# The last projection tile takes its feature blocks in another order, and attention's first score units run inside it

## What is computed

```python
h = rms_norm(x, norm_mix_g)
proj = h @ w_in                      # attention q,k,v (512 each); delta-rule q,k,v,z (512 each); gates
a_out = rms_norm(chunked_band_attention(rms_norm(a_q), rms_norm(a_k), a_v, rel_bias))   # 8 heads of 64
d_q, d_k, d_v = silu(causal_conv4(d_qkv))
o = gated_delta_rule(l2norm(d_q), l2norm(d_k), d_v, beta, alpha)      # 4 heads of 128, serial over chunks
d_out = rms_norm(o) * silu(z)
x = x + concat(a_out, d_out) @ w_out
h = rms_norm(x, norm_ffn_g)
x = x + (silu(h @ w_gate) * (h @ w_up)) @ w_down                      # hidden width 2816
```

## Time and profile before

| what | us |
| --- | --- |
| median of 3 runs | 1337.23 |
| lowest and highest | 1332.9 and 1340.54 |
| the profiled execution, its device time | 1330.42 |
| its span in the profile | 1328.7 |
| mean granted TensorE clock | 0.994 of full speed |

### The profile page before, as it was taken

How to read it: one execution, slowest core, us unless ns; L and a number is a source line. 1 busy time by engine, 2 the same in 40 slices (tenths; PEclk the granted TensorE clock), 3 DMA queues, 4 the chain that set the end, 5 groups by cost and what they waited for, 6 DMA issues and landing times.

```text
span 1328.7 us, 18375 instructions
## 1 busy us (share of the span) xinstructions
PE 1284.2 (97%) x6940; PEld 1072.0 (81%) x6940; DVE 745.0 (56%) x1033; ACT 577.9 (43%) x928; POOL 750.6 (56%) x516
## 2 busy tenths in 40 slices
PE   7999999999989989899988999999999999999999
PEld 7888888888878768888867877888888888788887
DVE  6455654536526667745479675664556557344552
ACT  5577655562136654552253323333333233464441
POOL 4332455633229992223068979888787894474541
PEclk9999999999999999999989999999999999999999
DMA  5611355431251004633111534334444336986663
GB/s 207 244 43 36 101 155 145 133 97 32 52 174 45 2 16 143 219 128 115 64 64 64 181 152 166 137 126 182 182 183 154 151 147 214 333 274 200 198 196 144
DMA packets 77807, 186.11 MB, mean 140 GB/s; under 512 B 20680, under 2 KB 24848, under 8 KB 70680
## 3 DMA queue, kind: packets, MB, share of 16 engines
q1 hardware_dynamic: 72144, 180.71, 40.1%
q10 hardware_dynamic: 5576, 4.23, 1.1%
HBM read 130.59 MB, written 56.94 MB: 141 GB/s over the span
## 4 chain that ended last, share of the span: by engine, by line
PE 75%; POOL 7%; DVE 6%; ACT 4%; DMA 4%; issue 3%; SPq 1%; DVEq 0%; ACTq 0%; POOLq 0%
PE ps L1988 24%; PE ps L340 20%; PE ps L2013 13%; PE ps L351 6%; POOL SX L841 2%; PE ps L1820 2%; PE ps L1852 1%; DMA RAWD<-w_down 1%; PE ps L1912 1%; PE ps L1835 1%; PE ps L325 1%; PE ps L1801 1%; POOL WR L740 1%; DMA RAB<-down_t 1%; POOL WX L740 1%
## 5 line engine op out<-in xcount | busy, mean ns | idle before, releaser
L340 PE MATMUL ps<-HT,SPLIT 128*128 128x512 f32 (+1 forms) x1488 | 329.1, 379 | 0.4 <-POOL SPLIT L290 0.4
L340 PEld LDWEIGHTS ps<-HT,SPLIT 128*128 128x128 f32 x1488 | 265.9, 189 | 49.7 <-issue 0.5
L2013 PE MATMUL ps<-S,HI 128*128 128x512 f32 x616 | 190.0, 390 | 1.6 <-POOL S L885 1.3
L885 POOL TENSOR_TENSOR S<-RAB,S 128x512 fp32r<-128x512 f32 x77 | 106.8, 1390 | 95.2 <-ACT S L1056 95.0
L288 POOL CAST SPLIT<-RAW 128x1024 fp32r<-128x1024 f32 x31 | 33.5, 1080 | 186.9 <-PE ps L340 181.9
L2013 PEld LDWEIGHTS ps<-S,HI 128*128 128x128 f32 x616 | 115.5, 188 | 26.5 <-issue 1.7
L1988 PE MATMUL ps<-HI,WR 128*128 128x512 f32 x368 | 119.6, 395 | 5.5 <-ACT UV L1021 5.4
L2013 PE MATMUL ps<-S,LO 128*128 128x512 f32 x308 | 119.8, 389 | 0.0
L1529 DVE TENSOR_TENSOR LO<-RAB,HI 128x512 fp32r<-128x512 f32 x77 | 65.4, 859 | 94.5 <-ACT HI L1053 94.4
L1988 PE MATMUL ps<-S,WR 128*128 128x512 f32 x504 | 117.8, 389 | 0.0
L1988 PE MATMUL ps<-HI,WX 128*128 128x512 f32 x336 | 110.4, 390 | 4.2 <-DVE UV L1467 2.0
(11 more groups left out here) (262 smaller groups left out, 2496.7 us busy)
## 6 DMA issues: line engine op xcount, KB each, us to landing
hidden<-HB SPq DMA_DIRECT2D x11, 1792.0 KB, 6.6
RAB<-hidden SPq DMA_DIRECT2D x77, 256.0 KB, 3.2
RAW<-units SPq DMA_DIRECT2D x37, 512.0 KB, 4.0
RAWG<-w_gate SPq DMA_DIRECT2D x11, 1024.0 KB, 10.9
RAWU<-w_up SPq DMA_DIRECT2D x11, 1024.0 KB, 5.0
RAWD<-w_down SPq DMA_DIRECT2D x11, 1024.0 KB, 8.9
down_t<-RAWD SPq DMA_DIRECT2D x11, 1024.0 KB, 3.9
RAB<-down_t SPq DMA_DIRECT2D x44, 256.0 KB, 3.6
```

Of the source, the lines that this page charges most:

```text
L340: mm = pe.matmul(ps[:, bank + a // HALF, a % HALF:a % HALF + width], w, right[other][:, k, a:a + width], start=(k == 0 and part == 0 and o ...
L885: pool.tensor_tensor(down_b(q, 1), RAB[:, q % RAWS, 1, :], down_b(q, 0).bitcast(F32), ALU.subtract).then_inc(R["b_lo"], 1)
L2013: mm = pe.matmul(ps[:, bank + t, :], down_a(q, part)[:, t * P:(t + 1) * P], down_b(q, other), start=(p == 0 and i in (1, 6, 5, 7) and part ...
```

## The change

It has five parts. (1) `columns_unit` takes an `order` of the feature blocks, and can raise a semaphore after block 7. (2) The last tile is made by a new function `project_last` with the order 3, 4, 5, 6, 7, 0, 1, 2; scores(0) goes ahead of block 0 and scores(1) ahead of block 1, and the semaphore `room` goes up after block 7. (3) DVE begins attention at `room`. (4) ScalarE copies the last tile from PSUM after the exponentials of unit 1, in place of a Silu ahead of attention, and applies Silu in place (SBUF to SBUF) after attention's last PT copy; PE waits for the banks between scores(2) and turn(0). (5) DVE's `att_acc(dve, 2)` moves from ahead of the STATE memset to behind the two masked copies of `dn_dve(0)`, and the first use of the z tiles waits for the late Silu.

```diff
-        def columns_unit(pe, slot, bank, right, first=0, end=T, between={}):
+        def columns_unit(pe, slot, bank, right, first=0, end=T, between={}, order=range(KT), read=None):
...
-            for k in range(KT):
+            for k in order:
...
-                                           start=(k == 0 and part == 0 and other == 0),
-                                           stop=(k == KT - 1 and part == 1))
+                                           start=(k == order[0] and part == 0 and other == 0),
+                                           stop=(k == order[-1] and part == 1))
+                if read is not None and k == KT - 1:
+                    mm.then_inc(read, 1)
...
-                for t in range(Z0, NPROJ):
+                for t in range(Z0, NPROJ - 1):
...
+                    if v == 1:
+                        act.wait_ge(unit_used, U_OUT)
+                        act.activation(proj_banks(NPROJ - 1), bank_pair(slot_of(NPROJ - 1), 4), ACT.Copy).then_inc(banks_free, 1)
...
+                act.wait_ge(banks_free, U_OUT + BANKS0)
+                act.activation(proj_tile(NPROJ - 1), proj_tile(NPROJ - 1), ACT.Silu).then_inc(proj_final, 1)
                 act.wait_ge(A["ao"], NPAIR * NT + AO0)
                 att_square(act, 3)
...
+                if m == 0:
+                    dve.wait_ge(proj_final, SQ0 + 1)
...
                 if m >= 1:
                     dn_dve_r(dve, m - 1)
+                else:
+                    att_acc(dve, 2)
...
-                dve.wait_ge(unit_used, U_OUT)
+                dve.wait_ge(A["room"], 1)
...
                 dve.wait_ge(A["ao"], NPAIR * NT + AO0)
-                att_acc(dve, 2)
                 dve.memset(STATE[:, :, :], 0.0).then_inc(S["st"], 4)
...
+            def project_last(pe):
+                t = NPROJ - 1
+                pe.wait_ge(split_done, U_TILE + t + 1)
+                pe.wait_ge(banks_free, U_TILE + t + 1)
+                columns_unit(pe, slot_of(t), 4 + 2 * slot_of(t), HTP, 0, T,
+                             {0: lambda: att_scores(pe, 0), 1: lambda: att_scores(pe, 1)},
+                             (3, 4, 5, 6, 7, 0, 1, 2), A["room"]).then_inc(unit_used, 1)
...
-                for t in range(SDV + 1, NPROJ):
+                for t in range(SDV + 1, NPROJ - 1):
...
-                att_scores(pe, 0)
-                att_scores(pe, 1)
-                pe.wait_ge(banks_free, U_OUT + BANKS0)
+                project_last(pe)
                 for v in range(NV):
                     if v + 2 < NV:
                         att_scores(pe, v + 2)
+                    if v == 0:
+                        pe.wait_ge(banks_free, U_OUT + BANKS0)
                     att_turn(pe, v)
```

More of the change, by code:

```diff
@@ L364, in hymba_block @@
         A = {n: sem("att_" + n) for n in
-             ("acc", "gt_turned", "masked", "scores", "biased", "prob", "turned", "pt0", "pt1", "pv", "inv", "scaled", "ao",
+             ("room", "acc", "gt_turned", "masked", "scores", "biased", "prob", "turned", "pt0", "pt1", "pv", "inv", "scaled", "ao",
               "sq", "sums", "ln", "rs", "mix")}
```

## The result

| | median us | lowest to highest | runs |
| --- | --- | --- | --- |
| before | 1335.75 | 1332.6 to 1340.54 | 6 |
| changed | 1326.1 | 1324.67 to 1326.65 | 6 |

The ratio is 0.9932, with a 95% interval of 0.9911 to 0.9953. By it the change takes 9.1 us (6.3 to 11.9) off. I had said 6.1, just outside that interval. The measured time lies inside the stated range, near its fast end. The profiled execution of the changed kernel took 1324.67 us, span 1322.9, against a span of 1328.7 before: 5.8 us. So the two profiles differ by less than the medians do, and both numbers have to be explained.

The account below looks back on a forecast made before the run. PE, busy in 97% of the span, bounds the kernel, so time comes only from its waits or slow stretches. Gains of 4.2 + 1.9 = 6.1 us take the median from 1337.23 to 1331.1 us, range 1325.5 to 1337.

Parts of the forecast that it names:

- First turn: Projection to attention: with scores inside the last tile, scores(3) ends 4.2 us earlier (bounds 2.5 and 4.7).
- a pause of 0.47 for the copy: Projection to attention: PE was to stand 0.5 us before turn(0) for ACT's copy of the last tile.
- idle weight loads: Last projection tile: PE's weight loads idle 0.17 us at each of two switches between scores and projection.
- both PE and POOL move by the same time: Attention: both engines gain 4.2 us at its start, so its end moves by as much.
- Second turn: Attention to delta rule: later sum of squares brings first TT addition 2.0 us earlier; 1.9 taken, bounds 0.7 and 2.8.
- The lock: Attention to delta rule: DVE's sum of squares is blocked until POOL's subtract ends; without this, gain near 3 us.
- 1.3 us to spare: Attention to delta rule: ACT's square could come 1.3 us later, against a possible 1.2 us delay from table switching.
- 1324.3 forecast: Whole kernel: the profiled execution's 1330.42 us less the gain of 6.1 us.
- (a): First turn pays, second doesn't, as clock falls or DVE's sum ends later: gain 3 to 4.9 us; chance 0.15.
- (b): Delta rule: a load of UT keeps its old time and swallows the shift; gain 0 to 2 us; chance 0.12.
- (c): Attention to delta rule: DVE's sum waits for POOL, TT begins 5.9 us later; 1.7 us slower overall; chance 0.05.
- (d): Clock stays up at second turn and switches cost nothing: gain 4.7 + 2.8 = 7.5 us or more; chance 0.13.

Follow-up runs that it names:

- e7: Changed kernel with scores(0) and scores(1) each one block later in the last tile: 1327.23 us, ratio to before 0.9953.
- e6: Changed kernel with POOL's second weight unit held until DVE's sum of squares is done: 1324.94 us, ratio to before 0.9930.
- e2: Kernel before with only DVE's sum of squares moved behind the two masked copies: 1329.75 us, ratio to before 0.9966.
- e4: Changed kernel with DVE's sum of squares one step later, behind both additions to TT: 1324.24 us, ratio to before 0.9929.
- e12: Kernel before run once more without any edit, a single run for a second profile: 1334.09 us.
- e3: The changed kernel run again without further edit, beside its parts on the same chip: 1325.39 us, ratio to before 0.9934.
- e11: e1 plus 12 matmuls of the identity that nobody reads, in PE's pause from attention to delta rule: 1323.72 us, ratio to before 0.9924.
- e1: Changed kernel with DVE's sum of squares put back ahead of the STATE memset: 1330.85 us, ratio to before 0.9976.
- e5: Kernel before with 9 and 12 unread identity matmuls in PE's pauses at the two turns: 1331.36 us, ratio to before 0.9990.
- e9: e4 with the loads of x's first four rows behind all of the delta rule's loads: 1320.04 us, ratio to before 0.9898.
- e10: Kernel before with the loads of x's first four rows behind all of the delta rule's loads: 1330.42 us, ratio to before 0.9967.
- e8: e4 with the loads of x's first four rows moved behind the delta rule's loads for tile 6: 1324.18 us, ratio to before 0.9927.

## Why the prediction was right, and where it was short

**The terms of the sum.** First turn: predicted 4.2, measured 4.19 at scores(3) and 4.20 at the last output copy. The path in between was right too: table load at 380.38, POOL 0.2 late, a pause of 0.47 for the copy (I had 0.5), and idle weight loads of 0.35 or so at a change instead of 0.17. The prediction that both PE and POOL move by the same time held. e7 shows that the lead pays.

Second turn: predicted 2.0 (1.9 taken), measured 2.20 between the last output copy and the TT addition. The lock was named rightly; e6 shows it. The sum did not wait for the Silu. The load ends at 490.45, Silu begins at 490.46, and the square begins 0.08 after the last output copy, as before. The Trainium skill (ScalarE: Activation LUTs, What ACT_TABLE_LOAD costs) has a drain of some 1.38 us with each switch of tables; an estimate from that page would have the square 1.2 us late. The trace disagrees. (The square ended 1.6 us before POOL's subtract, 492.75 against 494.38; I had given it 1.3 us to spare.) Of the exclusive hold of the shared ports (the Trainium skill, SBUF — State Buffer, SBUF: two separate sides) e2, e4 and e6 show the same as the page: 2.08 us under POOL's subtract, 1.21 us without it.

Both terms together were 6.1, and 6.4 us are what the first TT addition moved.

**What was short.** First, the second turn's term stopped at the TT addition. From there to L1945 the kernel before took 4.42 us, partly at the low clock, and the changed kernel takes 3.57. So the second turn was worth 3.05 us at that point, and not the 1.9 taken, nor at most 2.8. That is the term of the sum that was mis-sized. The sentence "If the clock still falls, `att_sum` runs partly in it and some 1 us of the 2.0 is lost" looked only for what the clock could take away, and not for what it gives back when it doesn't fall. Second, I counted the clock only inside the two turns and only as it stood in one execution. Between two executions the difference is larger, and goes on in the delta rule. Markers of three profiles, in us:

| | before | before again (e12) | changed | before - changed | e12 - changed |
| --- | --- | --- | --- | --- | --- |
| last output copy ends | 495.8 | 495.6 | 491.6 | 4.2 | 4.0 |
| first TT addition | 501.8 | 501.6 | 495.4 | 6.4 | 6.2 |
| first `osum` | 516.1 | 516.9 | 508.9 | 7.2 | 8.0 |
| last `osum` | 590.8 | 593.1 | 582.5 | 8.3 | 10.6 |
| last up or gate product | 1113.4 | 1115.2 | 1105.7 | 7.7 | 9.5 |
| span | 1328.7 | 1332.4 | 1322.9 | 5.8 | 9.5 |

The paths of the turns end with the second line. The 2 to 4 us between it and the last `osum` are clock and UT: 0.8 and 1.8 us up to the first `osum`, low clock; then PE waits 1.0 and 1.1 us less for UT in the changed kernel, and e12 has one low stretch more. Behind the last `osum`, where the edits change nothing, 2.5 and 1.1 us of the lead are lost again: from there to the end the changed kernel's first profile has 740.4 us, against 737.9 before, 739.2 in e12 and 737.8 in e3. In the 158 timed runs of the kernels, within each kernel, 0.001 of mean clock goes with 0.99 us of time (1.5 us of scatter beside it). Before has 0.9905, the changed kernel 0.995: by this slope some 4.4 of its 9 us go with the clock. (Part of that is inside the 6.4, since the low clock at the turns was in the rows.) e11 against e1 speaks for a cause and not a companion: matmuls that nobody reads gave 6.9 us (4.4 to 9.4), of which 0.0040 of clock would be 3.9 by the slope. e5 against before speaks for less: 0.0033 of clock would be 3.3 us, and it got 1.3. So the size of the clock's share stays open.

**The base.** I wrote that the profiled execution lies 6.8 us below the median and subtracted the same 6.1 from both. About half of the 6.8 was clock: 0.994 against 0.9905 is 3.5 us by the slope. The rest was the scatter of three runs: the 60 runs of the kernel before beside the experiments have medians of 1333.9 to 1334.5, and the six of the result 1335.75. So 1.5 of the 5.0 us between 1331.1 and 1326.1 are the base, and the rest is the gain. That the profiled execution itself landed within 0.4 us of the 1324.3 forecast is in part luck: it had lost 2.5 of the 8.3 us again by the end.

**The rivals.** (a), the clock falling again at the second turn, didn't come in any of the profiles of the changed kernel. It came in e7 (500.3 to 503.7 us), though PE's pauses at that turn are those of the changed kernel; so it can come there as well. (b), the shift swallowed at UT: the wait was 1.8 before, 1.5 and 3.0 in the two profiles of the changed kernel, so up to 1.2 us of it; e9 and e10 are too coarse to show it. (c), the sum of squares held until POOL is through, did not happen. (d), more than 7 us, had 0.13 and was nearest to the result. Of its two terms the clock that stays up at the second turn came (7.3 us at L1964); the first turn without any cost of a switch didn't.

**Chances.** It came out faster by over 0.5%, which had 0.43; within 0.5% had 0.52. With the first turn and the second each near its middle value, that hung on the clock.

**The low clock in the delta rule.** Seven times the clock fell between 530 and 570 us: twice in e1, once in e6, e7, e8, e10 and e12. PE is 90% to 100% busy in these stretches, so they seem to come from nowhere. But each stands right behind a wait of PE in the delta rule itself, of 1.87 to 2.86 us: for DVE's UT in e10, e12 and the first of e1, for the load of UT in the others. In the 3.4 us ahead of the fall PE had worked 0.8 to 1.6 us. So what came ahead of each is its own wait, and not the pause at the turn, 35 us or more earlier. Nor does every such wait bring one: behind 2.96 us in e3, 2.85 in e2 and 2.58 in e4 the clock stayed at 1.00. What stays open is what decides it from one execution to the next, and why three of the four profiles with the long second pause (before, e1, e10, e12) have such a stretch and only three of the other ten. The longest wait for DVE's UT is 1.7 to 2.2 us in those four and 0.95 to 2.0 in the others; nothing here tests whether that is the reason.

## What to carry to other kernels

Where two stages meet, the filling of the second one's pipeline can go inside the last tile of the first: order the tile so that the memory which the second needs comes free first. Count a pause of PE twice, once as time and once as clock, and look at the granted clock of many executions, not of one; a few matmuls that nobody reads are a quick test of the second part, though it needs many runs (e5 left it open). Where the clock is low, read what the engine did just ahead of that stretch and not in it. On an engine between two stages, put the operation whose reader comes last behind those that PE waits for.

## What the runs showed that I had not expected

- Filling one pause of 3.3 us, with 1.15 us of work around it, gave 6.9 us (e11 against e1; 4.4 to 9.4), more than its length, though DVE's next step came no earlier.
- The clock fell behind waits of PE of 1.9 to 2.9 us with work before and after them, and behind others as long it didn't.
- The kernel before scatters over 8.3 us (15 runs, 1330.46 to 1338.77, on the last chip), e9 over 4.7 (5 runs). Five runs are too few to call it steadier.
- 2 MB of loads in front of a 256 KB one made it land in 6.7 to 8.3 us; the other loads of that line in the delta rule take 2.5 to 4.6. Moving them was worth 4.4 us in the kernel before (2.5 to 6.1), at a place that the change had not touched, and about as much in e9, where the error is 3.8.
